# A bidirectional gated recurrence on TensorE: heads one at a time, or in pairs with the row halves by turns

## What is computed

```
bcum = cumsum(log_a)                  # log gates of the chunk's tokens
q_dec, k_inv = q * exp(bcum), k * exp(-bcum)
k_end = k * exp(btot - bcum)          # btot: the chunk's last bcum
att = where(mask, q_dec @ k_inv.T, 0)
o = att @ v + q_dec @ S               # S: the state before the chunk
S = exp(btot) * S + k_end.T @ v
```

## Time and profile before

| | |
|---|---|
| median of 3 runs | 2001.46 us (2001.36 to 2001.58) |
| the profiled execution | 1998.61 us |
| its span | 1997.3 us |
| PE busy | 1954.6 us, 15561 records |
| mean granted clock of TensorE | 0.995 |
| instructions | 37085 |

### The profile page before, as it was taken

The page is one execution under the profiler, slowest core; times in us unless marked ns, Lnnn a source line. Parts: engine busy times, 40 slices in busy tenths (PEclk is TensorE's granted clock), DMA queues, the critical chain, the costliest instruction groups (busy, mean ns, idle before and its releaser), DMA issues.

```text
span 1997.3 us, 37085 instructions
## 1 busy us (share of the span) xinstructions
PE 1954.6 (98%) x15561; PEld 1876.9 (94%) x15561; DVE 1385.9 (69%) x2291; ACT 1018.3 (51%) x1702; POOL 35.3 (2%) x56
## 2 busy tenths in 40 slices
PE   7999999999999999999999999999999999999998
PEld 7999988899999999988889999989999998899998
DVE  6776555578776677655558877677888556788854
ACT  5444455565444444445565544456555445565543
POOL 0000000000000000000000000030000003000000
PEclk9999999999999999999999999999999999999999
DMA  6775323246675577532235877343445544354553
GB/s 252 260 274 225 127 85 106 80 147 239 253 281 189 189 259 282 211 113 98 95 107 181 288 270 284 107 151 133 169 160 199 190 161 142 124 180 155 203 182 122
DMA packets 51246, 363.23 MB, mean 182 GB/s; under 512 B 6566, under 2 KB 8006, under 8 KB 9224
## 3 DMA queue, kind: packets, MB, share of 16 engines
q1 hardware_dynamic: 51080, 360.86, 51.2%
HBM read 359.78 MB, written 1.05 MB: 181 GB/s over the span
## 4 chain that ended last, share of the span: by engine, by line
PE 87%; DVE 7%; ACT 3%; DMA 2%; issue 1%; SPq 0%; DVEq 0%; ACTq 0%
PE bank L425 24%; PE bank L426 24%; PE bank L427 24%; DVE w_lo L1493 2%; PE bank L625 1%; DMA raw_a<-in_weights 1%; ACT w_hi L1028 1%; PE bank L461 1%; PE bank L457 1%; PE bank L458 1%; PE bank L517 1%; DVE full L1535 1%; PE bank L576 1%; PE bank L689 1%; PE bank L739 1%
## 5 line engine op out<-in xcount | busy, mean ns | idle before, releaser
L425 PE MATMUL bank<-xn_hi,w_hi 128*128 128x256 f32 (+1 forms) x2480 | 717.2, 289 | 5.9 <-DVE w_lo L1493 5.9
L427 PE MATMUL bank<-xn_lo,w_hi 128*128 128x256 f32 (+1 forms) x2480 | 706.8, 285 | 0.0
L426 PE MATMUL bank<-xn_hi,w_lo 128*128 128x256 f32 (+1 forms) x2480 | 705.2, 284 | 0.0
L425 PEld LDWEIGHTS bank<-xn_hi,w_hi 128*128 128x128 f32 x2480 | 466.6, 188 | 18.1 <-issue 16.1
L1493 DVE TENSOR_TENSOR w_lo<-raw_a,w_hi 128x1024 fp32r<-128x1024 f32 (+1 forms) x282 | 356.8, 1269 | 178.2 <-ACT w_hi L1028 177.4
L427 PEld LDWEIGHTS bank<-xn_lo,w_hi 128*128 128x128 f32 x2480 | 466.9, 188 | 0.1
L426 PEld LDWEIGHTS bank<-xn_hi,w_lo 128*128 128x128 f32 x2480 | 466.0, 188 | 1.1
L1493 DVE TENSOR_TENSOR w_lo<-raw_b,w_hi 128x1024 fp32r<-128x1024 f32 (+2 forms) x280 | 354.2, 1267 | 156.1 <-ACT w_hi L1028 155.2
L1028 ACT ACTIVATE w_hi<-raw_a 128x1024 fp32r<-128x1024 f32 (+1 forms) x282 | 306.3, 1088 | 242.5 <-PE bank L427 188.5
L1028 ACT ACTIVATE w_hi<-raw_b 128x1024 fp32r<-128x1024 f32 (+2 forms) x280 | 304.3, 1088 | 227.9 <-PE bank L427 195.0
L425 PE MATMUL bank<-h_hi,w_hi 128*128 128x272 f32 (+1 forms) x704 | 202.0, 287 | 0.0
(11 more groups left out here) (321 smaller groups left out, 3087.4 us busy)
## 6 DMA issues: line engine op xcount, KB each, us to landing
raw_b<-in_weights SPq DMA_DIRECT2D x123, 1024.0 KB, 4.8
raw_a<-in_weights SPq DMA_DIRECT2D x121, 1024.0 KB, 4.8
ada_raw<-in_ada_w SPq DMA_DIRECT2D x48, 1024.0 KB, 4.9
raw_a<-in_weights SPq DMA_DIRECT2D x16, 1408.0 KB, 5.8
raw_b<-in_weights SPq DMA_DIRECT2D x16, 1408.0 KB, 5.7
raw_a<-in_weights SPq DMA_DIRECT2D x2, 1152.0 KB, 5.1
raw_a<-in_weights SPq DMA_DIRECT2D x2, 640.0 KB, 4.0
cst<-in_const SPq DMA_DIRECT2D x1, 1152.0 KB, 9.2
```

Source lines behind the costliest of these rows:

```text
L425: pe.matmul(o, wh, xh, start=start, stop=False)
L426: pe.matmul(o, wl, xh, start=False, stop=False)
L427: return pe.matmul(o, wh, xl, start=False, stop=stop)
```

## The change

The second part of the recurrence takes heads in pairs. The scores of a pair go to bank 2 (head on rows 0 to 63) and bank 3 (rows 64 to 127), both directions side by side, the two heads by turns; the scores among meta tokens go to bank 4, one head's ahead of the rest and the other's behind it and behind a wait of TensorE on its own mark. VectorE masks all four tables in one step. The outputs of the two heads go to banks 2 and 3, state products by turns; the sums of squares go to bank 4. The second head's square follows the first head's root on ScalarE. A pair takes four steps where two heads took six, so the second part is done at unit 25.

The log gates' first tile is cleared to 128 rows by VectorE before ScalarE writes its 16 rows, and L576 multiplies all 128 rows (the constant's rows beyond 16 meet zeros).

```diff
+def meta_att(j, d):
+
+    return slice(T + META * (2 * j + d), T + META * (2 * j + d) + META)
...
                 for b, col in ((2, C_CUM[d]), (3, C_END[d])):
                     take(b)
                     for t, (c0, n) in enumerate(TILES):
-                        m = pe.matmul(bank[b][:, c0:c0 + n], c.la[0:n, t, d * 256 + p * P:d * 256 + p * P + P],
-                                      cst[0:n, col:col + n], start=True, stop=True)
+                        m = pe.matmul(bank[b][:, c0:c0 + n], c.la[:, t, d * 256 + p * P:d * 256 + p * P + P],
+                                      cst[:, col:col + n], start=True, stop=True)
...
-        for h in range(GLA_H):
-            p, hr = h // 2, slice(64 * (h % 2), 64 * (h % 2) + 64)
-            for d in range(2):
-                i, b = 2 * d + p, 2 + d
+        live = LIVE[l]
+        for p in range(2):
+
+            heads = [(b, 2 * p + b - 2, slice(64 * (b - 2), 64 * (b - 2) + 64)) for b in (2, 3)]
+            for b in (2, 3, 4):
                 take(b)
-                for c0, n in LIVE_TILES[l]:
-                    m = pe.matmul(bank[b][0:n, c0:c0 + n], c.kinv[hr, i, c0:c0 + n], c.qdec[hr, i, c0:c0 + n], start=True, stop=True)
-                m.then_inc(*k.up("gla_mm", ("att", l, h, d)))
-                free[b] = [("gla_v", ("att", l, h, d))]
-            yield
-            pe.wait_ge(*k.at("gla_v", ("att", l, h, 1)))
-            if h:
-                pe.wait_ge(*k.at("gla_v", ("normed", l, h - 1)))
+
+            def meta(j):
+                for d in range(2):
+                    keys, queries = (z[heads[j][2], 2 * d + p, 0:META] for z in (c.kinv, c.qdec))
+                    m = pe.matmul(bank[4][0:META, meta_att(j, d)], keys, queries, start=True, stop=True)
+                return m
+
+            if live == TA:
+                meta(0).then_inc(*k.up("gla_mm", ("meta", l, p)))
+            for c0, n in TILES[1:]:
+                for d in range(2):
+                    for b, _, hr in heads:
+                        m = pe.matmul(bank[b][0:n, d * SEQ + c0 - META:d * SEQ + c0 - META + n], c.kinv[hr, 2 * d + p, c0:c0 + n],
+                                      c.qdec[hr, 2 * d + p, c0:c0 + n], start=True, stop=True)
+            if live == TA:
+
+                pe.wait_ge(*k.at("gla_mm", ("meta", l, p)))
+                m = meta(1)
+            m.then_inc(*k.up("gla_mm", ("att", l, p)))
+            yield
+            pe.wait_ge(*k.at("gla_v", ("att", l, p)))
             for c0, n in LIVE_TILES[l]:
                 t = TILES.index((c0, n))
-                vt = c.vtok[0:n, t, h * P:(h + 1) * P]
-                todo = []
-                for d in range(2):
-                    todo.append((bank[4][:, c0:c0 + n], vt, c.att[2 * (h % 2) + d][0:n, c0:c0 + n]))
-                    for s, ch in enumerate(AFTER[d]):
-                        if CHUNKS[ch][0] == t:
-                            cs = slice(CHUNK_COL[ch], CHUNK_COL[ch] + CHUNKS[ch][2])
-                            todo.append((bank[4][:, cs], c.states[hr, 2 * d + p, s, :], c.qdec[hr, 2 * d + p, cs]))
-                todo.sort(key=lambda z: z[2].shape[0] != n)
-                for q, (o, lh, rh) in enumerate(todo):
-                    m = pe.matmul(o, lh, rh, start=q == 0, stop=q == len(todo) - 1, skip_group_check=True)
-            m.then_inc(*k.up("gla_mm", ("o", l, h)))
-            yield
-            pe.wait_ge(*k.at("gla_a", ("square", l, h)))
-            take(2)
-            pe.matmul(bank[2][:, LIVE[l]], c.ones, c.sq[:, LIVE[l]], start=True, stop=True).then_inc(*k.up("gla_mm", ("sum", l, h)))
-            free[2] = [("gla_a", ("root", l, h))]
-            yield
-        free[4] = [("gla_v", ("normed", l, GLA_H - 1))]
+                for b, h, _ in heads:
+                    for d in range(2):
+                        pe.matmul(bank[b][:, c0:c0 + n], c.vtok[0:n, t, h * P:(h + 1) * P], c.att[2 * (b - 2) + d][0:n, c0:c0 + n], start=d == 0,
+                                  stop=False, skip_group_check=True)
+                states = [(d, s, slice(CHUNK_COL[ch], CHUNK_COL[ch] + CHUNKS[ch][2])) for d in range(2) for s, ch in enumerate(AFTER[d])
+                          if CHUNKS[ch][0] == t]
+                for d, s, cs in states:
+                    for b, _, hr in heads:
+                        m = pe.matmul(bank[b][:, cs], c.states[hr, 2 * d + p, s, :], c.qdec[hr, 2 * d + p, cs], start=False,
+                                      stop=(d, s, cs) == states[-1], skip_group_check=True)
+            m.then_inc(*k.up("gla_mm", ("o", l, p)))
+            yield
+            for b, h, _ in heads:
+                pe.wait_ge(*k.at("gla_a", ("square", l, h)))
+                take(4)
+                pe.matmul(bank[4][:, live], c.ones, c.sq[:, live], start=True, stop=True).then_inc(*k.up("gla_mm", ("sum", l, h)))
+                free[4] = [("gla_a", ("root", l, h))]
+                free[b] = [("gla_v", ("normed", l, h))]
+                yield
...
             la = c.la[0:n, t, :]
+            if t == 0:
+                act.wait_ge(*k.at("gla_v", ("clear", l)))
             act.wait_ge(*k.at("gla_mm", ("z", l, t)))
...
+        def square(h):
+            act.activation(c.sq[:, live], bank[2 + h % 2][:, live], ACT.Square).then_inc(*k.up("gla_a", ("square", l, h)))
+
+        for p in range(2):
+            yield
+            act.wait_ge(*k.at("gla_mm", ("o", l, p)))
+            square(2 * p)
+            yield
+            for h in (2 * p, 2 * p + 1):
+                act.wait_ge(*k.at("gla_mm", ("sum", l, h)))
+                if h:
+                    act.wait_ge(*k.at("gla_v", ("normed", l, h - 1)))
+                inverse_root(c.gate[:, 0, live], bank[4][:, live], 1.0 / GLA_DV, "gla_a", ("root", l, h))
+                if h % 2 == 0:
+                    square(h + 1)
+                act.wait_ge(*k.at("gla_v", ("gated", l, h)))
+                act.activation(c.a_hi[:, h, live], c.full[:, 0, live], ACT.Copy).then_inc(*k.up("x_hi", ("a", l, h)))
+                yield
...
     def log_gates(l):
+        dve.memset(c.la[:, 0, :], 0.0).then_inc(*k.up("gla_v", ("clear", l)))
...
+        for p in range(2):
+            dve.wait_ge(*k.at("gla_mm", ("att", l, p)))
             for d in range(2):
-                o = c.att[2 * (h % 2) + d]
-                dve.wait_ge(*k.at("gla_mm", ("att", l, h, d)))
-                if live == TA:
-                    dve.copy_predicated(o[0:META, 0:META], c.msk[0:META, d, 0:META], bank[2 + d][0:META, 0:META]).then_inc(*k.up("gla_v"))
-                dve.copy_predicated(o[:, META:T], c.msk[:, d, META:T], bank[2 + d][:, META:T]).then_inc(*k.up("gla_v", ("att", l, h, d)))
-            yield
-            yield
-            f = c.full[:, 0, live]
-            dve.wait_ge(*k.at("gla_a", ("root", l, h)))
-            if h:
-                dve.wait_ge(*k.at("x_lo", ("a", l, h - 1)))
-            dve.tensor_tensor(f, bank[4][:, live], c.gate[:, 0, live], ALU.mult).then_inc(*k.up("gla_v", ("normed", l, h)))
-            dve.wait_ge(*k.at("tile_a", ("silu_r", l)))
-            dve.wait_ge(*k.newest("gla_v"))
-            dve.scalar_tensor_tensor(out=f, in0=f, scalar=c.v1[:, V_GN + h:V_GN + h + 1], in1=c.r_act[:, h, live], op0=ALU.mult,
-                                     op1=ALU.mult).then_inc(*k.up("gla_v", ("gated", l, h)))
-            dve.wait_ge(*k.newest("gla_v"))
-            low(c.a_lo[:, h, live], f, c.a_hi[:, h, live], ("a", l, h))
-            yield
+                for j in range(2):
+                    o = c.att[2 * j + d]
+                    if live == TA:
+                        dve.copy_predicated(o[0:META, 0:META], c.msk[0:META, d, 0:META], bank[4][0:META, meta_att(j, d)]).then_inc(*k.up("gla_v"))
+                    dve.copy_predicated(o[:, META:T], c.msk[:, d, META:T], bank[2 + j][:, d * SEQ:(d + 1) * SEQ]).then_inc(
+                        *k.up("gla_v", ("att", l, p) if d and j else None))
+            yield
+            yield
+            for h in (2 * p, 2 * p + 1):
+                f = c.full[:, 0, live]
+                dve.wait_ge(*k.at("gla_a", ("root", l, h)))
+                if h:
+                    dve.wait_ge(*k.at("x_lo", ("a", l, h - 1)))
+                dve.tensor_tensor(f, bank[2 + h % 2][:, live], c.gate[:, 0, live], ALU.mult).then_inc(*k.up("gla_v", ("normed", l, h)))
```

More of the change, by code:

```diff
@@ L1205, in gla @@
         live = LIVE[l]
-        for h in range(GLA_H):
+        def square(h):
+            act.activation(c.sq[:, live], bank[2 + h % 2][:, live], ACT.Square).then_inc(*k.up("gla_a", ("square", l, h)))
+        for p in range(2):
             yield
-            act.wait_ge(*k.at("gla_mm", ("o", l, h)))
-            act.activation(c.sq[:, live], bank[4][:, live], ACT.Square).then_inc(*k.up("gla_a", ("square", l, h)))
+            act.wait_ge(*k.at("gla_mm", ("o", l, p)))
+            square(2 * p)
             yield
-            act.wait_ge(*k.at("gla_mm", ("sum", l, h)))
-            if h:
```

(19 more changed lines are left out.)

## The result

| | before | changed |
|---|---|---|
| median | 2001.41 us (4 runs, 1994.83 to 2001.58) | 1982.85 us (4 runs, 1981.91 to 1984.02) |
| profiled execution, its span | 1998.61, 1997.3 us | 1982.28, 1981.0 us |
| mean granted clock in it | 0.995 | 0.995 |

The account below looks back on a forecast made before the run. TensorE (PE) was taken to bound the kernel. Savings of 5.2 + 3.2 + 5.5 + 2.4 + 4.2 less 0.7, 0.6 and 0.3 give 18.9 us, off the 2001.46 median: 1982.6 us, range 1979 to 1990.

Parts of the forecast that it names:

- pitch: TensorE records start 0.11 us apart; 64 or one moving columns cost no less than 128, as 128-column weights set the pace.
- row halves: On TensorE, products on rows 0 to 63 and 64 to 127 run side by side, each with its own pitch.
- A change of form: On TensorE, a visit to another number of rows or columns costs 0.1 to 0.2 us on top of its records.
- Padded log gates: Cumulative sums on 128 rows: 12 records take 1.27 instead of 1.92 us, eight times, 5.2 us saved; clears cost nothing.
- Scores and outputs: Taking heads in pairs saves 3.2 us in scores and 5.5 in outputs in layer 0, 2.4 and 4.2 in layer 1.
- Given back: Accidental overlap of row halves between heads goes once pairs fill both: 0.7 us lost in layer 0, 0.6 in layer 1.
- Masked copies: VectorE masks four tables in one piece; TensorE waits 0.3 us, once, at layer 1's first pair.
- no new PE wait but some tenths for att in layer 1: Sign of a right forecast: TensorE's list of waits gains only some tenths of a us, at layer 1's att products.
- VectorE becomes the bound of the pair: Rival, 12%: copies and scalings queue with softmax and weights on VectorE; 2 to 6 us lost, 1984.6 to 1988.6 us.
- Halves that gain nothing: Rival, 5%: alternating halves in scores and outputs share no time, only changes of form pay; 10.3 us less gain, 1992.9.
- share in part: Rival, 7%: every two records meant to share 0.11 us take 0.15; 3.4 us lost, 1986.0 us.
- a turn costs: Rival, 3%: some 92 head alternations in scores and state products cost 0.15 to 0.2 us each; 2007 to 2011 us.

Follow-up runs that it names:

- experiment 1: Changed kernel with the cumulative sums back on 16 rows, the clears kept; median 1986.93 us, ratio 0.9937 to the kernel before.
- experiment 9: Changed kernel with softmax ahead of the recurrence in units 20, 24 and 25, masked copies ahead of the gates; median 1978.99 us, changed kernel beside it 1984.58.
- experiments 5 to 9: Five versions of the changed kernel with masked copies ahead of the gates, all but one also with softmax earlier in some units; medians 1978.99 to 1984.93 us.
- experiment 8: Changed kernel with only the masked copies moved ahead of the gates on VectorE; median 1983.82 us.
- experiment 7: Changed kernel with softmax ahead of the recurrence in unit 24 only, behind head 2's sum, and masked copies ahead of the gates; median 1984.18 us.
- experiment 2: Changed kernel with scores and state products head after head instead of by turns, same banks; median 1989.27 us, ratio 0.9948 to the kernel before.

## Why the prediction was right, point by point

- **Bound, pitch, row halves**: right. The 15.9 us that PE's slots lost are the 16.0 of the runs. Sixteen records of two halves take the time of eight of one, to 0.01 us, in scores and states alike. **A change of form** is right in kind; a visit cost up to 0.29 us (experiment 1), and not 0.1 to 0.2.
- **Padded log gates, 5.2**: measured 4.64 (experiment 1: 4.7). This term was mis-sized. I took 1.27 us for twelve records by the row of one column; the records went at 0.11 each on average (1.34, my upper price). The clears were rightly costed at nothing.
- **Scores and outputs**: 1.47 us against 1.6 and 5.35 against 5.3 in layer 0; in layer 1 1.12 (952.71 to 953.83) against 1.09, and 4.03 and 3.93 against 3.8. PE's wait on its own mark shows nothing of its own: 0.2 us pass from L623's last start to L615 at 317.60, as for a change of form.
- **Given back, 0.7 and 0.6**: consistent with the sums. Layer 0's slots without late softmax (experiment 9) are 2.3 us shorter, so 5.58 + 2.34 = 7.92 against 8.0 predicted; layer 1's 5.67 stand against 5.7.
- **Masked copies, 0.3, once**: right in place and size, 0.35 (experiments 5 to 9), and on the chain. In layer 0 they end at 321.32, and PE comes at 321.67. "TensorEngine Tiling (Array Packing)" of the Trainium skill, section "PSUM Bottleneck", warned that emptying the banks may become the bottleneck. By these runs the masked copies cost 0.35 us beside the change's 16, and another order on VectorE gave that back (experiment 8).
- **The step that failed** is what the sum has for VectorE's other work: nothing. The sentence that the softmax maxima's "readers on PE come a unit later" speaks of the maxima behind the masked copies, and no wait shows there. Those behind the scaling of heads 0 and 2 (units 20 and 24) have no term at all. Their readers come a unit later too, but the scores that stood ahead of these readers had been moved away by the change itself. I asked what stands behind the new wait and not what the moved stage had been covering. It cost 0.88 + 0.92 us at the transposes and 0.61 behind them, 2.4 us in layer 0. The sign "no new PE wait but some tenths for att in layer 1" failed with it: 1.6 us of new waits are listed in layer 0 and 0.4 in layer 1, all for softmax tables or their transposed copies. So the rival *VectorE becomes the bound of the pair* came true in part, by another door than the copies, at the lower end of its 2 to 6 us.
- **The other rivals fell.** Halves that gain nothing or share in part would show in the starts (6 to 7 ns, then 0.105); a turn costs nothing measurable, as without turns it is 4.7 us slower. Two halves show a factor of 2.0 here, and not the 1.5 that the prediction estimated from the 3.07 that "TensorE: Matmul & The Clock Gate" of the Trainium skill, Part 3, section "Measured speedup vs the span model", gives for four row tiles; four tiles were not run.
- **The total** was closer than its parts, and that is luck: 1982.6 forecast and 1982.85 measured, but the sum was 3.0 us too high (0.55 padding, 2.4 softmax), and the medians lie 2.6 us further apart than the 16.0 us of work, as the clock falls more in some runs than in others. Over 40 and 16 runs the mean times are 2000.96 and 1983.99, 17.0 apart, at mean clocks of 0.9932 and 0.9936.

## What to carry to other kernels

Work that uses half of TensorE's rows should be issued by turns with work for the other half: in these shapes two streams cost what one costs. A visit to 16-row products cost 0.2 to 0.3 us here, so stages of one form belong together, if need be padded. When a stage is moved, list what it was covering at its old place, on every engine that feeds the next reader, and set their order anew: here a faster PE stage was worth 16 us, and the order of VectorE's and ScalarE's work in five units another 2.6 in the slots. After each such step look at the next wait in the list, since experiment 7 won next to nothing by mending the first of two.

## What was not expected of the hardware

- TensorE brings forward records of the other row half by itself, past three that stand ahead in the program (318.712 in experiment 2, 6 ns behind 318.706, and alike in all twelve groups of that run). "TensorE: Matmul & The Clock Gate" of the Trainium skill, Part 3, section "The mechanism", says that matmuls start and end strictly in program order. Across row halves these starts say otherwise, as did; the ends are modelled in the trace and say nothing on it.
- Records of 64 rows and 16 columns (L615) start 25 to 39 ns apart, not 0.11 us: a pitch set by the weights' 16 columns rather than 128 would fit, and wasn't tried.
- The clock falls at places that differ from execution to execution, and the same gap need not bring it. Windows of the changed kernel at the last outputs of attention of layer 0 (unit 34, where PE waits 0.9 us for ScalarE) and behind them, and then of experiment 9 at the same work:

```profile
401.40:404.90 3.50, 2.58 (x27) 1.41 (x27) 1.45 (x2) 3.50 (x7) 0.00 (x0) 0.99 0.00 0
404.90:408.30 3.40, 3.40 (x16) 3.40 (x17) 1.20 (x4) 3.06 (x4) 0.00 (x0) 0.50 0.77 275
```

```profile
398.90:402.40 3.50, 2.60 (x27) 1.44 (x27) 1.48 (x2) 3.50 (x7) 0.00 (x0) 1.00 0.00 0
402.40:405.80 3.40, 3.40 (x28) 3.40 (x28) 1.19 (x4) 3.31 (x5) 0.00 (x0) 1.00 0.78 267
```

  PE is busy for 2.6 of 3.5 us in both; the one falls to 1.2 GHz, the other goes on at 2.4. The fall of the earlier trace rows at 249.7 us was gone in the changed kernel's first profile and back in its third. What decides was not settled, nor whether experiment 9's higher mean clock would hold in more runs.
